# Another distance, modulo 256 bytes, between weights and moving tiles in each stage of a two-layer trunk

## The reference, cut to what matters

```python
def reference(x, ...):
    for i in range(DEPTH):                       # DEPTH = 2
        h = rmsnorm(x, norm1_g[i])
        x = x + (swa_sink_attention(h, w_qkv, w_o, ...) if i % 2 == 0 else retention(h, w_in, w_o))
        h = rmsnorm(x, norm2_g[i])
        x = x + conv_ffn(h, ffn_w_up[i], ffn_conv_w[i], ffn_conv_b[i], ffn_w_down[i])

def conv_ffn(h, w_up, conv_w, conv_b, w_down):   # D_FF = 2816
    u = causal_depthwise_conv(h @ w_up, conv_w) + conv_b
    a, b = jnp.split(u, 2, axis=-1)
    return (gelu(a) * b) @ w_down
```

## Time and profile before

| | before |
|---|---|
| median of 3 runs | 1266.78 us (1266.52 to 1267.2) |
| profiled execution: its own time | 1266.45 us |
| profiled execution: span | 1264.3 us |
| TensorE, matmuls | 1259.8 us busy, 5858 instructions |
| TensorE, weight loads | 1042.5 us busy, 5858 instructions |
| VectorE / ScalarE / GpSimd | 713.9 / 465.5 / 142.2 us busy |
| granted TensorE clock | 1.0 of full speed |

### The profile page before, as it was taken

How to read it: one execution, slowest core, us unless ns; L and a number is a source line. 1 busy time by engine, 2 the same in 40 slices (tenths; PEclk the granted TensorE clock), 3 DMA queues, 4 the chain that set the end, 5 groups by cost and what they waited for, 6 DMA issues and landing times.

```text
span 1264.3 us, 15565 instructions
## 1 busy us (share of the span) xinstructions
PE 1259.8 (100%) x5858; PEld 1042.5 (82%) x5858; DVE 713.9 (56%) x907; ACT 465.5 (37%) x655; POOL 142.2 (11%) x138
## 2 busy tenths in 40 slices
PE   9999999999999999999999999999999999999999
PEld 8777888888888888888888888888888888888887
DVE  6776586666763333545535634634676677663222
ACT  6664454444442233232233223223454444442120
POOL 3751300000000011402102101201000000000000
PEclk9999999999999999999999999999999999999999
DMA  7102232222222224322212222221232222222322
GB/s 244 68 34 84 87 106 100 100 100 100 92 76 92 92 91 153 128 77 99 100 67 75 100 100 75 100 75 59 100 109 100 100 96 83 90 78 96 107 91 89
DMA packets 22053, 120.43 MB, mean 95 GB/s; under 512 B 2696, under 2 KB 4000, under 8 KB 11264
## 3 DMA queue, kind: packets, MB, share of 16 engines
q1 hardware_dynamic: 20928, 117.59, 26.6%
q10 hardware_dynamic: 864, 1.98, 0.4%
q0 software_dynamic: 224, 0.35, 0.1%
HBM read 117.81 MB, written 2.11 MB: 95 GB/s over the span
## 4 chain that ended last, share of the span: by engine, by line
PE 99%; DVE 1%; POOL 0%; issue 0%; DVEq 0%
PE ps L1305 32%; PE ps L1307 32%; PE ps L1306 32%; PE ps L1425 1%; PE ps L1412 1%; PE ps L1403 1%; PE ps L1322 0%; PE ps L1343 0%; DVE w_lo L664 0%; PE ps L1386 0%; DVE mx L765 0%; POOL qs L1198 0%; DVE qss L737 0%; PE ps L1335 0%; PE ps L1376 0%; DVE qvar L740 0%
## 5 line engine op out<-in xcount | busy, mean ns | idle before, releaser
L1305 PE MATMUL ps<-h_hi,w_hi 128*128 128x512 f32 x960 | 375.3, 391 | 0.0
L1307 PE MATMUL ps<-h_hi,w_lo 128*128 128x512 f32 x960 | 373.6, 389 | 0.0
L1306 PE MATMUL ps<-h_lo,w_hi 128*128 128x512 f32 x960 | 373.5, 389 | 0.0
L664 DVE TENSOR_TENSOR w_lo<-raw,w_hi 128x2048 fp32r<-128x2048 f32 (+1 forms) x115 | 244.3, 2125 | 141.8 <-ACT w_hi L349 141.8
L349 ACT ACTIVATE w_hi<-raw 128x2048 fp32r<-128x2048 f32 (+1 forms) x115 | 202.6, 1762 | 212.1 <-PE ps L1307 212.1
L1307 PEld LDWEIGHTS ps<-h_hi,w_lo 128*128 128x128 f32 x960 | 180.2, 188 | 37.6
L1305 PEld LDWEIGHTS ps<-h_hi,w_hi 128*128 128x128 f32 x960 | 180.3, 188 | 37.4
L1306 PEld LDWEIGHTS ps<-h_lo,w_hi 128*128 128x128 f32 x960 | 180.3, 188 | 36.7
L1305 PE MATMUL ps<-g_hi,w_hi 128*128 128x512 f32 x352 | 136.9, 389 | 0.0
L1306 PE MATMUL ps<-g_lo,w_hi 128*128 128x512 f32 x352 | 136.9, 389 | 0.0
L1307 PE MATMUL ps<-g_hi,w_lo 128*128 128x512 f32 x352 | 136.9, 389 | 0.0
(11 more groups left out here) (162 smaller groups left out, 1434.0 us busy)
## 6 DMA issues: line engine op xcount, KB each, us to landing
raw<-in_w_up SPq DMA_DIRECT2D x44, 1024.0 KB, 4.8
raw<-in_w_ret SPq DMA_DIRECT2D x32, 1024.0 KB, 4.8
raw<-in_w_dn SPq DMA_DIRECT2D x32, 704.0 KB, 4.0
raw<-in_w_ao SPq DMA_DIRECT2D x4, 1024.0 KB, 5.3
raw<-in_w_q SPq DMA_DIRECT2D x3, 1024.0 KB, 4.8
x<-in_xT SPq DMA_DIRECT2D x8, 256.0 KB, 5.9
out<-x SPq DMA_DIRECT2D x7, 256.0 KB, 5.2
rbc<-root_mem SPq DMA_DIRECT2D x6, 256.0 KB, 3.0
```

What stands on the lines that cost most here:

```text
L664: nc.vector.tensor_tensor(w_lo[:, s, 0:cols], raw[:, s, 0:cols], w_hi[:, s, 0:cols].bitcast(F32), ALU.subtract).then_inc(w_lo_ok, 1)
L1305: nc.tensor.matmul(dst, st[0], mv[0], start=start, stop=False)
L1306: nc.tensor.matmul(dst, st[0], mv[1], start=False, stop=False)
L1307: return nc.tensor.matmul(dst, st[1], mv[0], start=False, stop=stop)
```

## The change

Empty tiles (`space`) are put between operands. Nothing else changes: each engine's instructions are the same ones in the same order before and after, except that their operands stand at other addresses.

```diff
+        def space(name, floats, scope=ctx):
+            scope.enter_context(nc.sbuf_tensor(f"space_{name}", [P, floats], F32))
...
         raw = sb("raw", [P, 2, UW])
+        space("w_hi", 48)
         w_hi = sb("w_hi", [P, 2, UW], F32R)
+        space("w_lo", 8)
         w_lo = sb("w_lo", [P, 2, UW], F32R)
+        space("gain", 8)
         gain = sb("gain", [P, 4, KT])
...
+        space("a_hi", 48, scope=att)
         a_hi = sb("a_hi", [P, KT, S], F32R, scope=att)
+        space("a_lo", 8, scope=att)
         a_lo = sb("a_lo", [P, KT, S], F32R, scope=att)
+        space("kto", 8, scope=att)
...
+        space("g_hi", 40, scope=ffn)
         g_hi = sb("g_hi", [P, FT, S], F32R, scope=ffn)
+        space("g_lo", 40, scope=ffn)
         g_lo = sb("g_lo", [P, FT, S], F32R, scope=ffn)
...
-        p_hi = sb("p_hi", [P, PT, S], F32R, scope=ret)
-        p_lo = sb("p_lo", [P, PT, S], F32R, scope=ret)
+        p_hi = sb("p_hi", [P, PT * S + 8], F32R, scope=ret)[:, 4:4 + PT * S].rearrange("p (t s) -> p t s", s=S)
+        p_lo = sb("p_lo", [P, PT * S + 64], F32R, scope=ret)[:, 52:52 + PT * S].rearrange("p (t s) -> p t s", s=S)
         sg = sb("sg", [P, RV_T, S], scope=ret)
         o_hi = sb("o_hi", [P, RV_T, S], F32R, scope=ret)
+        space("o_lo", 40, scope=ret)
         o_lo = sb("o_lo", [P, RV_T, S], F32R, scope=ret)
+        space("csr", 16, scope=ret)
```

## The result

The changed kernel takes 1293.16 us (median of 4 runs, 1292.84 to 1293.99) against 1266.94 us for the kernel before (4 runs, 1266.52 to 1267.2). The ratio is 1.0209, with a 95% interval of 1.0197 to 1.022: about 26 us slower. The forecast was 1252 us, faster, with a range of 1225 to 1276 us; both its sign and its range were wrong.

What follows compares the result with a forecast made beforehand. The prediction took TensorE's matmul pitch to bound the kernel; 4896 matmuls saving 3 ns each gave 14.7 us off 1266.45 us, 1251.8, predicted as 1252 us, with a range of 1225 to 1276 us.

Steps and rivals of the forecast that it cites:

- What bounds the kernel: Whole kernel: TensorE is 99% of the chain of waits, so only its cost per matmul, the pitch of 226.7 ns, counts.
- What the change can act on: 4896 matmuls of 512 columns get a new distance between moving tile and loaded weights; each ns is 4.9 us.
- The control: Output of the attention and the retention's scores keep distance 0; the attention's output must stay at 226.7 ns.
- Is the 13.3 ns something that distance can change?: Step asking whether each matmul's time beyond its columns comes from weight load and stream disturbing each other; some gain, 0.48.
- 4896 x 3 ns: Term for the 512-column matmuls with a new distance: a third of 9 ns saved on each, 14.7 us less.
- The 9 ns: Overhead absent in the retention's 128-column values matmul, taken as the most a matmul could save: 44 us in all.
- The second sign: Behind the transpose of `root_row` eight pitches take 231.3 ns each at the same distance; only load timing against streams differs.
- The 231.3 ns: Unsettled pitch behind the transpose of `root_row`, 4.6 ns above the settled one; used as the worst case.
- The bounds: For the 4896 matmuls: best 9 ns less each, 1222 us; worst 4.6 ns more each, 1289 us.
- Slower: Rival: distance 0 is the good one; up to 4.6 ns more a matmul, 22.5 us, 1289 us; chance 0.21.
- No effect: Rival: the 13.3 ns belong to the fp32r matmul itself, wherever its weights are loaded from; 1266.5 us; chance 0.31.
- Its twin: Case placed with no change: the pitch returns to 226.7 ns by itself from any distance; 1266.5 us, within the 0.31.

Runs made afterwards that it cites:

- e2_lo160: Kernel before with every hi operand (h, w, a, g, o) at 128 and every lo operand at 160 modulo 256: 1289.52 us, ratio 1.0179.
- r1_short: Kernel before, loading 64 of 128 weight columns in the down-projections and 32 of 128 in the output of the retention: 1272.72 us.
- n1_narrow: Kernel before with down-projection streams of 256 columns in the first layer and 384 in the second, instead of 512: 1197.49 us, making only part of the output.
- m1: Kernel before with h at 144, g at 112 and o at 96 modulo 256, hi like lo, w at 128: 1295.79 us.
- m3: Kernel before with h at 0, g at 176 and o at 224 modulo 256, hi like lo, w at 128: 1293.15 us.

## Why the prediction was wrong

**What bounds the kernel.** Right. TensorE decides alone, and the pitch of its matmuls is the whole of the change: the stages' pitches add up to the 26.4 us.

**What the change can act on.** Nearly right. The 4896 matmuls carry 26.2 of the 26.4 us. The control was not one: I took the output of the attention to be untouched since its distance is 0, and it lost 0.7 us. `e2_lo160` shows why, a jump between hi and lo is enough.

**Is the 13.3 ns something that distance can change?** This step failed: "The overhead is full as soon as a stream is at least as long as the weight load beside it ... and mostly absent in a stream of 128 columns ... That is how two readers would look that disturb each other while both run." `r1_short` halved and quartered the loads, and the pitch rose. `n1_narrow` found 13.3 ns at 256 and 384 columns at distance 0, as at 512. I had read as a disturbance what no run could lower. The term "4896 x 3 ns" less was in fact 5.4 ns more. The 9 ns it came from were read from one matmul of three: 220 ns is the mean of L1305 at 128 columns, while L1306 and L1307 there have 276 and 274 ns, and the pitches are 57.5, 112.5 and 113.5 ns. One load follows the other at some 110 ns there, so loads limit that stage, it is never in the steady state of the others, and it carries no conclusion for them.

**The second sign**, "if time counts, distance may", was right, and I drew the wrong consequence from it. The 231.3 ns of the earlier trace rows with the same operands at the same distance was the trace's own sample of what a matmul costs out of its steady state, and it was worse than 226.7. The fourteen other distances lie around it, 228.9 to 238.0 ns with a mean of 233.5. The profile held a price of the right size and sign, and I used it only as the upper bound. That both are the same thing isn't shown: behind the transpose the pitches jump between 224 and 236 ns and return to 226.7 after nine matmuls.

**The bounds.** The lower one, 9 ns less, has no run behind it: no stage of 512 columns had a steady pitch under 226.7 ns in any kernel of the study. The upper one, 4.6 ns more, was too low: the steady pitches of the two main stages went to between 231 and 233.3 ns, 4.3 to 6.6 ns more, and other distances reach 11.3. The stated range ended lower still, at 2 ns a matmul, so it left out most of the slower case. At the measured mean of 5.4 ns (26.2 us over 4896) the rival's own sum gives 1292.7 us.

**The rivals.** "Slower" had the mechanism, distance 0 as the favourable one, and 0.21. Its price of 1289 us was 4 us short. "No effect" fell, and with it the reading of the earlier trace rows: a single load from another distance, or a short one, leaves its neighbour at 0.22 to 0.23 us, yet a steady stream of such loads does not. One odd load says nothing of many in a row. Its twin, that the pitch settles by itself from any distance, fell as well, but for the first head of `m1`. The rule of the Trainium skill that I weighed there (TensorE: Matmul & The Clock Gate, "Step-by-step: what each phase is for"), that loading the next weights takes no read bandwidth from the running matmul, agrees with `r1_short` in that a shorter load gave no time back (230.0 ns), but can't explain that the place of the weights changes the pitch by up to 11.3 ns. There the measurement decides.

**What is shown and what stays open.** Shown: at distance 0 modulo 256 bytes with no jump, and with loads of 128 columns, the queue settles at columns plus 13.3 ns in every long stage; moving one tile against the other by 4 to 128 bytes, moving the lo half of either alone (16 to 64 bytes were tried), or shortening the load, ends that in all stages but one (`m1`, first head) and gives 2 to 11 ns more; moving all tiles together to 64 changes nothing. The pitch then isn't fixed by the addresses modulo 256 alone, for the same stage has two values in the changed kernel, in `m3` and in `m1`. Open: what selects between these values, where on the chip the two readings meet, if they do, and what the 13.3 ns are. No run looks inside.

## What to carry to other kernels

This was seen in one kernel, with fp32r operands and a weight load before every matmul. Where TensorE is the bound and its stream is dense, compare the pitch of a long steady stage with columns over clock. If it is already one constant in all stages, keep the operands' places modulo 256 bytes alike, hi and lo, weights and moving tiles, and check them after every new tile or odd size. A pitch that varies between stages or layers with the same shapes can be the sign that they aren't alike. And when a trace shows the same instruction out of its steady state, give its price there real weight in the forecast for a change that may disturb the state; here it was nearer than the gain that I had argued for.

## What the runs showed of the hardware that was not expected

- 4 bytes between the starts of weights and moving tile changed the pitch of a 512-column fp32r matmul from 226.7 to 238.0 ns; no other distance tried cost as much.
- Loads of 64 or 32 columns instead of 128 made the matmuls beside them slower, 230.0 and 231.7 ns against 226.7.
- The same stage at the same addresses modulo 256 settled at 231 ns in one layer and at 233.3 ns in the other (changed kernel), and at 226.7 ns in one head and 233.3 ns in the next (`m1`, +16 bytes).
